# RWKV chunks: the key scores' mask moved to VectorE, straight out of PSUM, and one scan moved behind the first level

## The reference

```python
def rwkv7_scan(r, decay, k, v, a_vec, b_vec):
    # S_t = S_{t-1} diag(decay_t) + (S_{t-1} a_t) b_t^T + v_t k_t^T ;  y_t = S_t r_t
    def step(state, inp):
        r_t, w_t, k_t, v_t, a_t, b_t = inp
        sa = jnp.einsum('bhvk,bhk->bhv', state, a_t)
        state = state * w_t[:, :, None, :] + sa[..., None] * b_t[:, :, None, :] + v_t[..., None] * k_t[:, :, None, :]
        y = jnp.einsum('bhvk,bhk->bhv', state, r_t)
        return state, y
    ...
y = rwkv7_scan(r, decay, k, v, -kk, kk * a)
```

## Time and profile before

| | |
|---|---|
| runs, median of 3 | 1818.29 us |
| runs, lowest and highest | 1818.24 and 1820.73 us |
| the profiled execution's own time | 1822.12 us |
| its span in the trace | 1820.2 us |
| TensorE busy | 1745.1 us, 96% |
| VectorE, ScalarE, GpSimd busy | 538.4, 525.7, 168.2 us |
| mean granted TensorE clock | 0.991 |

### The profile page before, as it was taken

One profiled execution on the slowest core, in us unless ns is written; L12 is line 12 of the kernel. 1 busy time (PEld: TensorE's weight loads), 2 busy tenths in 40 slices (PEclk: granted clock), 3 DMA queues, 4 the chain that ended last, 5 costly groups with the idle time before them and its releaser, 6 DMA issues.

```text
span 1820.2 us, 23627 instructions
## 1 busy us (share of the span) xinstructions
PE 1745.1 (96%) x9138; PEld 832.0 (46%) x9138; DVE 538.4 (30%) x987; ACT 525.7 (29%) x941; POOL 168.2 (9%) x208
## 2 busy tenths in 40 slices
PE   8999999999999999989999999999999999989898
PEld 4555777455533333333334444686433333333333
DVE  2154555422422231312223005212242232222123
ACT  3245342523322222122223004513332222222213
POOL 2000351110100000000002000311100000000000
PEclk9999999999999999999999999999999999999999
DMA  7210100363499999999994113106399999999995
GB/s 198 93 47 1 48 2 2 105 245 139 147 412 395 420 421 421 422 420 421 421 377 147 48 61 124 47 0 238 124 360 355 421 421 421 422 421 421 421 422 223
DMA packets 98391, 466.48 MB, mean 256 GB/s; under 512 B 23423, under 2 KB 25583, under 8 KB 49178
## 3 DMA queue, kind: packets, MB, share of 16 engines
q1 hardware_dynamic: 87392, 450.98, 62.0%
q0 software_dynamic: 4608, 7.92, 1.2%
q10 hardware_dynamic: 6330, 6.71, 1.1%
HBM read 468.15 MB, written 6.29 MB: 261 GB/s over the span
## 4 chain that ended last, share of the span: by engine, by line
PE 71%; DMA 23%; DVE 2%; ACT 2%; issue 1%; SPq 0%; DVEq 0%; ACTq 0%
PE ps L1132 65%; DMA W<-in_moe_w 23%; PE ps L1341 2%; PE ps L1867 1%; PE ps L1830 1%; ACT MK L900 0%; DMA xin<-in_x 0%; PE ps L1576 0%; PE ps L1278 0%; PE ps L1368 0%; PE ps L1782 0%; DVE gcs L2289 0%; DVE gsn L2320 0%; PE ps L1741 0%; PE ps L1733 0%
## 5 line engine op out<-in xcount | busy, mean ns | idle before, releaser
L1132 PE MATMUL ps<-W,xgT 128*64 128x512 f32 x1984 | 458.2, 599 | 11.7 <-DMA W<-in_moe_w 10.2
L1132 PE MATMUL ps<-HT,W 128*128 128x512 f32 (+2 forms) x896 | 336.7, 537 | 4.8 <-DVE XT L2448 2.2
L1132 PE MATMUL ps<-W,act 128*64 128x512 f32 x992 | 236.6, 611 | 28.7 <-DMA W<-in_moe_w 28.7
L1132 PEld LDWEIGHTS ps<-W,xgT 128*64 128x64 f32 x1984 | 131.1, 136 | 260.0 <-issue 239.7
L1132 PEld LDWEIGHTS ps<-HT,W 128*128 128x128 f32 (+1 forms) x896 | 167.1, 190 | 162.5 <-issue 147.3
L1088 ACT ACTIVATE ysb<-ps 32x512 f32<-32x512 f32 x248 | 146.1, 589 | 262.4 <-PE ps L1132 260.3
L2448 DVE TENSOR_TENSOR XT<-ps,XT 128x512 f32<-128x512 f32 x248 | 159.8, 686 | 170.5 <-PE ps L1132 170.5
L2442 DVE TENSOR_TENSOR act<-ps,sl 128x256 f32<-128x256 f32 x64 | 27.0, 422 | 473.3 <-ACT sl L1081 473.3
L1077 ACT ACTIVATE hs<-ps 128x512 f32<-128x512 f32 x64 | 38.2, 597 | 429.3 <-PE ps L1132 429.3
L1132 PE MATMUL ps<-spread,ysb 64*128 64x256 f32 x992 | 139.8, 401 | 2.7 <-DVE ysb L2468 1.7
L1132 PEld LDWEIGHTS ps<-W,act 128*64 128x64 f32 x992 | 65.8, 139 | 155.7 <-issue 113.0
(11 more groups left out here) (430 smaller groups left out, 1583.9 us busy)
## 6 DMA issues: line engine op xcount, KB each, us to landing
W<-in_moe_w SPq DMA_DIRECT2D x372, 1024.0 KB, 17.5
W<-in_od_w_in SPq DMA_DIRECT2D x6, 2048.0 KB, 8.8
W<-in_ev_w_in SPq DMA_DIRECT2D x3, 2048.0 KB, 8.1
W<-in_xa_wq SPq DMA_DIRECT2D x2, 2048.0 KB, 8.5
W<-in_xa_wo SPq DMA_DIRECT2D x2, 2048.0 KB, 12.9
WY<-in_moe_w SPq DMA_DIRECT2D x4, 1024.0 KB, 8.4
hrows<-hk ACTq DMA_DIRECT2D x8, 512.0 KB, 4.9
HT<-in_moe_w SPq DMA_DIRECT2D x4, 1024.0 KB, 7.9
```

The source lines that it names most:

```text
L1132: return te.matmul(o, l, r, start=first, stop=last)
```

## The change

VectorE gets a function `mask_keys(c)` that multiplies each key score by `tri` straight from its bank into MK. It is called first in each chunk, ahead of the small copy of Ep (`fc`, in chunks 0 to 2) and of `weighted_keys(0)` (in chunk 3). ScalarE's four copies per chunk (semaphore `ck_kraw`) and GpSimd's four products per chunk are gone. TensorE's wait at level 1 is for `ck_kmask` now, and the wait for it at level 3 is gone. In chunks 1 and 2 `cumulate` moves from ahead of level 1 to behind it, where chunk 0 has it already.

```diff
@@ gpsimd @@
-                def mask_keys(c, i):
-                    q, r = SCORES[i]
-                    part = MK[:, 2 * q:2 * q + 2, r, :, :].rearrange("p j x t -> p j (x t)")
-                    pool.wait_ge(s["ck_kraw"], 4 * c + i + 1)
-                    g.tensor_tensor(part, part, tri[:, :, :].rearrange("p x t -> p (x t)").unsqueeze(1).broadcast_to([P, 2, 2 * CH]),
-                                    ALU.mult).then_inc(s["ck_kmask"], 1)
...
-                    mask_keys(c, 0)
-                    mask_keys(c, 1)
-                    mask_keys(c, 2)
-                    mask_keys(c, 3)
@@ scalar @@
-                    for i, (q, r) in enumerate(SCORES):
-                        act.wait_ge(s["ck_kmat"], 4 * c + i + 1)
-                        sc.activation(MK[:, 2 * q:2 * q + 2, r, :, :].rearrange("p j x t -> p j (x t)"),
-                                      ps[:, 4 + 2 * q + r, :].rearrange("p (j n) -> p j n", j=2), ACT.Copy).then_inc(s["ck_kraw"], 1)
@@ tensor @@
                         if l == 1:
-                            pe.wait_ge(s["ck_kraw"], 4 * c + 4)
+                            pe.wait_ge(s["ck_kmask"], 4 * c + 4)
...
                         if l == 3:
-                            pe.wait_ge(s["ck_kmask"], 4 * c + 4)
@@ vector @@
+                def mask_keys(c):
+                    for i, (q, r) in enumerate(SCORES):
+                        dve.wait_ge(s["ck_kmat"], 4 * c + i + 1)
+                        ve.tensor_tensor(MK[:, 2 * q:2 * q + 2, r, :, :].rearrange("p j x t -> p j (x t)"),
+                                         ps[:, 4 + 2 * q + r, :].rearrange("p (j n) -> p j n", j=2),
+                                         bcast(tri[:, :, :].rearrange("p x t -> p (x t)").unsqueeze(1), [P, 2, 2 * CH]),
+                                         ALU.mult).then_inc(s["ck_kmask"], 1)
...
                 for c in range(NCH):
                     following = slice((c + 1) * CH, (c + 2) * CH)
+                    mask_keys(c)
                     if c + 1 == NCH:
...
                         st.then(ve.tensor_copy(fc.unsqueeze(2), Ep[:, :, CH - 1:CH]))
-                        if c:
-                            cumulate(following)
...
-                        if l == 1 and c == 0:
+                        if l == 1 and c + 1 < NCH:
                             cumulate(following)
```

More of the change, by code:

```diff
@@ L364, in trunk @@
             "shifted", "lora_done", "lora_taken", "kk_max", "pre_a", "pre_p", "post_v", "post_a", "post_p", "gate_done", "gate_in", "bonus_sum", "bonus_p", "bonus_in", "half_done", "half_in",
-            "ck_scan", "ck_mid", "ck_cs", "ck_rh", "ck_sn", "ck_exp", "ck_el", "ck_kt", "ck_vc", "ck_turned", "ck_tok", "ck_mat", "ck_masked", "ck_kmat", "ck_kraw", "ck_kmask", "ck_sd", "ck_y", "ck_y_in", "ck_s",
+            "ck_scan", "ck_mid", "ck_cs", "ck_rh", "ck_sn", "ck_exp", "ck_el", "ck_kt", "ck_vc", "ck_turned", "ck_tok", "ck_mat", "ck_masked", "ck_kmat", "ck_kmask", "ck_sd", "ck_y", "ck_y_in", "ck_s",
             "iv_id", "u_first", "u_mid", "u_cross", "u_part", "iv_u", "iv_ul", "iv_v", "iv_x", "akv_done", "akv_in", "u_done", "u_in",
```

## The result

The changed kernel takes 1822.41 us (median of 12 runs, 1819.74 to 1826.30), the kernel before 1819.14 us (12 runs, 1816.87 to 1823.17). The ratio is 1.0018, with a 95% interval from 1.0011 to 1.0025: 3.3 us slower, 2.0 to 4.5, which is within the 0.2% that I took as the bound of no change. I forecast 1819.9 us, +1.6, in the range 1816.4 to 1823.5; the time lies in it, near its upper end. The profiled execution took 1822.57 us, span 1820.8, against 1822.12 and 1820.2 before; these two alone would show 0.5 us, and the part on why the prediction was right takes this pair apart.

A forecast was written before the change was run, and what follows sets the result against it. TensorE, busy 96% of the span, was taken as the bound, with at most 1.92 us idle to win. Terms 0.39 + 0.06 + 0.06 + 1.09 = +1.60 us on 1818.29 gave 1819.9 us, range 1816.4 to 1823.5.

The forecast's parts named there:

- The wait that takes ScalarE's place: Level 1, chunks 0 to 2: TensorE's second product waits for VectorE's four masks, 2.49 us; +0.39, +0.06, +0.06 us.
- KKt in chunk 3: Chunk 3: the masks delay VectorE's weighted_keys(0), so TensorE's first bonus product starts 1.09 us later, paid in full.
- cumulate hidden behind level 1's follower: Chunks 1 and 2: cumulate, 1.83 us, makes level 2's placing 0.34 us late, hidden by a projection product; 0 us.
- the 1.4 to 1.8 us that I gave as the sign: Chunks 1 and 2: scans of this length behind level 1 would show the forecast right, level 3 starting without waiting for XI.
- The rival in which it doesn't fit: Chunks 1 and 2: cumulate takes 3.46 us, stalling level 2 by 1.5 us each; +4.6 in all, 1822.9 us; chance 0.04.
- No overlap of four masks: VectorE, every chunk: four masks take 2.76 us, 0.27 more each; sum +2.7, 1821.0 us; chance 0.05.
- The scans' length: Cumulate in chunks 1 and 2: with no GpSimd product beside them, scans take their median 0.41 us, four plus copy 1.83.
- The step that failed: After the chunks: their shift of +1.60 us passes to the kernel's end in full, with nothing added.
- the case among the rivals: Outside the chunks: later stages with transfers swallow or multiply the shift; not priced beyond the spread 1818.24 to 1822.12; chance 0.07.

The follow-up runs named there:

- keys_first: Changed kernel with VectorE's product KKt ahead of the masks in chunk 3; one execution 1819.39 us, stage (the chunks' stretch) 134.67 us against 135.08.
- shared_masks: Changed kernel with ScalarE copying banks 1 and 3 for GpSimd, VectorE masking 2 and 4, KKt first in chunk 3; 1818.37 us, ratio 0.9999 to the kernel before.
- cumulate_alone: Kernel before with only cumulate moved behind level 1 in chunks 1 and 2; one execution 1820.64 us, stage 133.76 us, 0.23 over the kernel before.
- shared_again: Second timing of the kernel that splits the masks between ScalarE with GpSimd and VectorE; 1818.04 us, ratio 0.9997 to the kernel before.
- masks_twice: Changed kernel with VectorE doing all four masks of each chunk twice, signalling only the second time; 1851.77 us, ratio 1.0166 to the kernel before.

## Why the prediction was right in the chunks and short by half outside

- **The wait that takes ScalarE's place.** Right. Four masks took 2.47 to 2.48 us (I said 2.49), TensorE's second product is released by VectorE in chunks 0 to 2, +0.33, +0.03, +0.06 against 0.39, 0.06, 0.06.
- **KKt in chunk 3.** Right: +1.16 against 1.09, TensorE idle for 1.38 us. keys_first shows that 0.41 of it is the order; behind the masks alone TensorE still stands idle for 0.92 us there.
- **cumulate hidden behind level 1's follower.** Right, and with more room than I gave it: 1.33 + 0.17 us against 1.83 (the scans a little under the 1.4 to 1.8 us that I gave as the sign), AKV still idle for 0.83 us ahead. The rival in which it doesn't fit had no GpSimd product to meet. Two of my readings there are loose: the first placing stands at 234.37 in the row, where I took it as due at 234.43, and the rival uses 236.42 where the part on cumulate has 236.35. With the row's figure cumulate is 0.40 us late, still under the slack of 0.48.
- **No overlap of four masks.** Wrong as the row said: 0.60 apart in a run of four too. The Trainium skill says in "VectorE: DVE Perf Modes", The DRAIN you can't avoid, that the next op does not start until the pipe is empty; read by itself, and with the 0.69 us that one mask takes in shared_masks, this gives an estimate of 2.76 us, and the trace has 2.48. The same section goes on that a next op that is not held starts earlier, which my prediction left out; the trace agrees with this.
- **The scans' length.** They are 380 to 425 ns in all four places of the changed kernel, where they were up to 1431, and 1.96 us for four in cumulate_alone beside GpSimd's masks. The Trainium skill, "SBUF — State Buffer", Who interferes with whom, says that a VectorE instruction with two SBUF inputs contends with a GpSimd instruction that reads SBUF; these numbers agree with it.

```profile
L2025 DVE TENSOR_TENSOR_SCAN CS<-ones,SGt x16: 380/397/425, 58.0 to 266.3; 128x128 f32<-128x128 f32 x16
```

- **The step that failed** is the last of the sum: "All that follows the chunks starts from their end, so I let the shift pass to the end in full". It passed, and brought another 1.7 us with it. I had the case among the rivals, as a scatter to both sides with a chance of 0.07, and could not price it. The runs put 2.9 us on a pure delay of 1.72, by the ratio (1.8 to 4.0), and the profiles point to the place of at least a part: the first routing, 15.6 and 16.2 us before, 17.1 to 17.2 in all four profiles that lie 1.55 to 1.72 us later. The rest of the distance from 1819.9 is the base: the median of before was 1818.29 in the three runs shown and 1819.14 in twelve, and my sum on that one gives 1820.7.

How well the parts add up shows in the profiled executions. With the kernel before run again as the standard (1819.74 us), the changed kernel's 1822.57 is 2.83 more: stage 1.55, first routing 1.55, second 0.0, start of the stage 0.04, and -0.3 for all else. Against the first profile of the kernel before (1822.12) it is only 0.45 more, since there the first routing gives +1.0 and the second -1.6: this is why a single pair misleads. **The transfers, which I had named as what could multiply a shift, have no part in it that the profiles show.** Take from each execution's time the start of the stage, the stage, the two routings and the products that were added: what is left is 1465.3 us in both profiles of the kernel before, 1465.0 in both of the changed kernel, 1465.2 and 1465.6 with the delay, and 1464.3 to 1465.9 in all 14.

**Left open:** which share of the 1.7 us is the first routing's in the average run, and which the second's, isn't shown, since one profile stands for each set of runs; nor what decides where the clock falls, since cumulate_alone has the late fall almost without a delay. The second routing took 18.8 to 18.9 us in three profiles (before, shared_again, masks_twice), 15.6 in one and 17.2 or 17.3 in the others, which doesn't follow the result.

## What to carry to other kernels

When a queue of small reads is on the chain, moving it whole to another engine only changes who is waited for; count how long the new owner takes for the whole queue, and split it if neither engine keeps pace. Look in every place at what the added instructions stand ahead of: in chunk 3, which made three quarters of the cost in the stage, the product of 0.74 us behind the masks was 0.41 us of it, and the masks' own length on one engine the rest. And below 0.2%, judge such an edit by the length of its own stage in the profile, which repeated to 0.01 us here, and test the rest with a pure delay of the same length before blaming the edit.

## What the runs showed of the hardware

- In masks_twice, TensorE waits of 3.43, 3.15, 3.15 and 3.90 us were each followed by a stretch at half clock (about 7 us, behind the last one 34.1), and 10 us of added work became 30. Behind the waits of 0.63 to 1.38 us in the changed kernel's stage the clock stayed at 1.00.
- The time from the start of the trace to the stage came in three lengths: 186.4 to 186.9 us, 188.1 to 188.3, and once 189.4. The granted clock of TensorE in the first 30 us tells them apart (1.00, 0.94, and once 0.89). Of the kernel before, and of the kernel before with the delay (whose first 186 us are the same program):

```profile
0.00:30.00 30.00, 22.89 (x70) 0.94 1.06 282
```

```profile
0.00:30.00 30.00, 23.59 (x73) 1.00 1.08 282
```

That alone spreads equal kernels: the two profiles of the shared masks, the same kernel, start their stage at 189.42 and 186.40 us, 3.0 apart.
- The two routings took 31.0 to 35.2 us together in 14 profiles whose code there is the same, by where the clock fell in them, and whether it did.
